# Attention scores of two heads issued as a pair: NSA and MoBA steps in a new order

## The chip, the cores and the metric

The kernel runs on one core of a Trainium2 chip. The metric is device time in microseconds (us). Three runs of the kernel before took 2022.54, 2023.51 and 2023.94 us, median 2023.51. The profiled execution took 2022.18 us; the span that the profile covers is 2020.5 us of it.

## The reference

The program computes two transformer blocks on 512 tokens of width 1024 in float32. Block one has a mixer of 8 NSA heads and 8 MoBA heads, then a mixture of 32 experts; block two has differential attention (DA) and retention. Cut to the branches that the change touches:

```python
# NSA, selected branch; with 8 selection blocks and a top of 16, every causal key is selected
s = einsum('bghcd,bgcmd->bghcm', qc, ksel) * scale
s = s - sl * dist
p = masked_softmax(s, dist >= 0)
o_sel = einsum('bghcm,bgcmd->bghcd', p, vsel)
# NSA, window branch: the same with kw, vw; the window of 512 covers all keys
return gc[..., 0:1] * o_cmp + gc[..., 1:2] * o_sel + gc[..., 2:3] * o_win
# MoBA, 8 heads, two key blocks of 256: causal attention over all keys
p = masked_softmax(concatenate([s_g, s_c]), concatenate([mask_g, mask_c]))
```

So in this kernel there are 16 causal attentions for NSA (8 heads, 2 branches) and 8 for MoBA, each with head width 64 and 512 queries.

## The kernel before, in words

A **step** is one block of 128 queries (row `i`, 0 to 3) of one head in one branch. It meets the first `i + 1` blocks of 128 keys. NSA has 64 steps and MoBA 32, numbered through (`st["at"]`). A step passes over three engines:

- TensorE (PE), `scores`: one matmul of 64 contracted partitions into one of three PSUM banks (`bank[n % 3]`), 128 to 512 columns wide. Queries and keys of a head lie in one half of the 128 partitions: `half` is 0 or 64. A float32 matmul shows as two records in the trace, so a step has two records of scores.
- VectorE (DVE), `dve_attend`: adds the bias and takes the row minimum in one pass (line 660), signal `s_bias`.
- ScalarE (ACT), `act_attend`: the exponential with its row sum (line 605), signal `s_exp`.
- PE, `turn`: transposes the probabilities, one block of 128 at a time (line 568), signal `t_done`. ACT copies them to SBUF (line 597), signal `t_ok`.
- PE, `values`: multiplies them with the values, one matmul a block (line 579), signal `o_done`.
- DVE, `accumulate`: reciprocal of the sum (line 641), in NSA times the gate (line 643), then the scaled addition into `omix` (line 648 in NSA, 651 in MoBA), signal `o_acc`.

Everything is written out by hand. `pe_attend` issues in its turn n: the scores of step n, the transposes of step n-2, the values of step n-3. `dve_attend` issues the bias of step m, then in NSA one piece of other work (`modulate_part`, line 629: an eighth of a chunk of the ada weights), then `accumulate` of step m-3. Both walk the lists `nsa_steps` and `moba_steps` in order. In the kernel before a head's four rows follow one another; heads of the two halves alternate head by head (0, 4, 1, 5, ... in NSA; even and odd in MoBA).

NSA steps are followed by the projections for MoBA (lines 395 and 403), then come the MoBA steps, the output projection (lines 789 and 798), the router, and the expert stage (lines 1426 and 1443), whose weights stream from HBM through a ring of 12 slots of 1 MB. In block two, `pe_da` issues the two score matmuls of a DA step (line 675), one in each half of the partitions, one directly behind the other.

Of the kernel before, what the change touches and what calls it, by code (L numbers as in the profile page):

```python
# [12 lines left out]
P = 128  # L13
S = 512
D = 1024
NT = S // P
# [3 lines left out]
HD = 64  # L20
HEADS = 8
# [52 lines left out]
def two_block_layer(nc, x, vec_rows_in, misc_in, ada_w, w_in, nsa_cmp_pos, nsa_cmp_w1, nsa_cmp_w2, w_out, router_w,  # L74
# [9 lines left out]
    with ExitStack() as ctx:  # L84
# [3 lines left out]
        def sem(name):  # L88
            return ctx.enter_context(nc.semaphore(name))

        bank = [ctx.enter_context(nc.psum_tensor(f"bank{i}", [P, 512], F32)) for i in range(8)]
# [17 lines left out]
        def room(at, shape, parts=P):  # L109
# [149 lines left out]
        s_done, s_bias, s_exp, t_done, t_ok, o_done, o_acc = (  # L259
            sem(n) for n in ("s_done", "s_bias", "s_exp", "t_done", "t_ok", "o_done", "o_acc"))  # L260
# [95 lines left out]
        at = norms = rs = 0  # L356
# [157 lines left out]
                    after[j["at"]]()  # L514


        nsa_steps, moba_steps, da_steps = [], [], []
        for br in range(2):
            for h in [0, 4, 1, 5, 2, 6, 3, 7]:
                half = HD * (h // 4)  # L520
                for i in range(NT):
                    nsa_steps.append(dict(
                        q=qkT[half:half + HD, h % 4, i * P:(i + 1) * P], k=qkT[half:half + HD, 4 + br, 0:P * (i + 1)],
                        v=lambda kt, br=br: vtok[:, kt, P * br:P * br + P], vw=HD, v0=half,
                        bias=bias8[:, h, S - P * (i + 1):S], blocks=i + 1,
                        over=nsa_gate[:, i, 3 * h + br + 1:3 * h + br + 2], dst=omix[:, i, HD * h:HD * h + HD], add=True))
        for h in range(HEADS):
            half = HD * (h % 2)
            for i in range(NT):
                moba_steps.append(dict(  # L530
                    q=qkT[half:half + HD, h // 2, i * P:(i + 1) * P], k=qkT[half:half + HD, 4 + h // 2, 0:P * (i + 1)],
                    v=lambda kt, h=h: vtok[:, kt, P * (h // 2):P * (h // 2) + P], vw=HD, v0=half,
                    bias=bias8[:, h, S - P * (i + 1):S], blocks=i + 1,
                    over=None, dst=omix[:, i, 512 + HD * h:512 + HD * h + HD], add=False))
        for h in range(4):
            for i in range(NT):
                da_steps.append(dict(
                    q=[qkT[HD * m:HD * m + HD, h, i * P:(i + 1) * P] for m in range(2)],
                    k=[qkT[HD * m:HD * m + HD, 4 + h, :] for m in range(2)],
                    v=lambda kt, h=h: vtok[:, kt, P * h:P * h + P],  # L540
                    bias=bias4[:, h, 384 - P * i:384 - P * i + S], dst=omix[:, i, P * h:P * h + P]))
        at = 0
# [7 lines left out]
        S_DA = O_MOBA + 2 * len(da_steps)  # L550

        def pe_attend(pe, steps, banks_free=None):
            def scores(st):
                n = st["at"]
                if n >= 3:
                    pe.wait_ge(s_bias, n - 2)
                pe.matmul(bank[n % 3][:, 0:P * st["blocks"]], st["q"], st["k"], start=True, stop=True)\  # L557
                  .then_inc(s_done, 1)

            def turn(st):  # L560
                n = st["at"]
                pe.wait_ge(s_exp, n + 1)
                if st is steps[0] and banks_free:
                    banks_free()
                if n >= 3:
                    pe.wait_ge(t_ok, n - 2)
                for b in range(st["blocks"]):
                    mm = pe.transpose(bank[3 + n % 3][:, b * P:(b + 1) * P], st["p"][:, b * P:(b + 1) * P],  # L568
                                      ident[:, :])
                mm.then_inc(t_done, 1)  # L570

            def values(st):
                n = st["at"]
                pe.wait_ge(t_ok, n + 1)
                if n >= 2:
                    pe.wait_ge(o_acc, n - 1)
                for b in range(st["blocks"]):

                    mm = pe.matmul(bank[6 + n % 2][:, 0:P], probT[n % 2][:, b * P:(b + 1) * P], st["v"](b),  # L579
                                   start=(b == 0), stop=(b == st["blocks"] - 1))  # L580
                mm.then_inc(o_done, 1)
            for n in range(len(steps) + 3):
                if n < len(steps):
                    scores(steps[n])
                if 2 <= n <= len(steps) + 1:
                    turn(steps[n - 2])
                if n >= 3:
                    values(steps[n - 3])
# [660 lines left out]
        def _(pe):  # L1249
# [86 lines left out]
            for g in range(2):  # L1336
                pe.wait_ge(c_ac, 5 + g)
                for i in range(NT):
                    mm = pe.matmul(bank[CMP_BANK[i]][:, SW * g:SW * g + SW], cmp_pT[:, g, P * i:P * i + P],
                                   vc_diag[:, g, :], start=True, stop=True)  # L1340
                    if g == 1:
                        mm.then_inc(c_pe, 1)

            pe_attend(pe, nsa_steps, lambda: pe.wait_ge(c_dv, C_O))
            pe.wait_ge(t_ok, O_NSA)
            pe.wait_ge(o_acc, O_NSA)
            pe_project(pe, moba_jobs,
                       after={moba_jobs[n]["at"]: lambda parts=parts: modulate(parts) for n, parts in MOD_AFTER.items()})
            pe.wait_ge(z_free, moba_jobs[-1]["at"] + 1)
            pe_attend(pe, moba_steps)  # L1350
            pe.wait_ge(o_acc, O_MOBA)
            pe_out(pe, 0, "w_out", 0)
# [736 lines left out]
```

## Time and profile before

| what | us |
|---|---|
| median of three runs | 2023.51 |
| profiled execution | 2022.18 |
| span in the profile | 2020.5 |
| NSA steps, from the first steady turn to the projections | 176.04 to 284.60 |
| MoBA steps | 389.13 to 442.50 |
| PE busy in the span | 1922.7 (95%) |
| DVE busy | 679.4 (34%) |
| ACT busy | 375.0 (19%) |

The PE row of the page is near 9 tenths nearly throughout. In a timeline row the second number is how long the group lasts by the profile, and the end of a matmul is modelled; the pace of an engine is read from one start to the next start. In the chain of waits a row's second number is the time that the row contributes to the chain, so these add up to elapsed time.

### The profile page before, as it was taken

To read this page: it belongs to the slowest core of one execution; us is meant where nothing else is said; L and a number is where in the kernel's file an instruction comes from. 1 tells how busy PE (TensorE), PEld (TensorE's weight loads), DVE (VectorE), ACT (ScalarE), POOL (GpSimd) and SP (SyncE) were. 2 spreads that over 40 slices of the span, in tenths; PEclk is the share of its full clock that TensorE was granted. 3 is DMA by queue.
4 is the path that set the end of the run, shared out by engine and by line. 5 is a ranking of instruction groups with operands and counts; after the bars stand their busy time and mean duration, and the time that the engine had idled before them with its cause. 6 is when DMAs were issued, how large, how long until landed. Compare 5 with 4: busy or idle time off the path is not lost.

```text
span 2020.5 us, 37108 instructions
## 1 busy us (share of the span) xinstructions
PE 1922.7 (95%) x15662; PEld 992.4 (49%) x15662; DVE 679.4 (34%) x1755; ACT 375.0 (19%) x821; POOL 192.3 (10%) x237
## 2 busy tenths in 40 slices
PE   5999999999799999999999998999999969989989
PEld 4486664764434434344434343434343434855854
DVE  6446767431412212121212121212121254176140
ACT  2214542250201101011101111111110112052010
POOL 1020000000002112012111111111111100000000
PEclk9979999999799999999999999999999989999999
DMA  9721223321289999999999999999999882100001
GB/s 303 219 80 54 73 78 110 132 93 63 75 317 382 393 397 400 397 396 391 398 398 393 399 395 397 402 387 369 391 395 401 339 267 90 63 1 1 1 0 42
DMA packets 144751, 498.97 MB, mean 247 GB/s; under 512 B 20787, under 2 KB 89513, under 8 KB 95433
## 3 DMA queue, kind: packets, MB, share of 16 engines
q1 hardware_dynamic: 122192, 464.81, 59.6%
q0 software_dynamic: 16448, 22.69, 5.3%
q10 hardware_dynamic: 5944, 9.09, 1.3%
q8 instruction: 125, 2.05, 0.4%
q14 instruction: 42, 0.34, 0.0%
HBM read 481.08 MB, written 17.96 MB: 247 GB/s over the span
## 4 chain that ended last, share of the span: by engine, by line
PE 83%; DMA 10%; DVE 4%; ACT 1%; issue 1%; SPq 1%; ACTq 0%; DVEq 0%
PE bank L1426 26%; PE bank L1443 12%; PE bank L395 10%; DMA ring<-in_exp_w_dram 9%; PE bank L403 8%; PE bank L798 6%; PE bank L557 3%; PE bank L579 3%; PE bank L568 2%; PE bank L1415 1%; PE bank L1407 1%; PE bank L769 1%; PE bank L379 1%; PE bank L1390 1%; DVE arena L745 1%; PE bank L1398 1%
## 5 line engine op out<-in xcount | busy, mean ns | idle before, releaser
L1426 PE MATMUL bank<-ring,arena 128*32 128x512 f32 x5568 | 646.6, 599 | 13.8 <-DMA ring<-in_exp_w_dram 11.7
L1426 PEld LDWEIGHTS bank<-ring,arena 128*32 128x32 f32 x5568 | 163.9, 110 | 327.4 <-issue 294.5
L1443 PE MATMUL bank<-ring,arena 128*32 128x256 f32 x5568 | 307.9, 379 | 7.7 <-DMA ring<-in_exp_w_dram 6.2
L1443 PEld LDWEIGHTS bank<-ring,arena 128*32 128x32 f32 x5568 | 181.8, 110 | 141.1 <-issue 22.0
L395 PE MATMUL bank<-hT,ring 128*128 128x512 f32 x448 | 210.3, 622 | 13.2 <-DVE hT L775 7.5
L1823 DVE COPY arena<-bank 128x12 f32<-128x12 f32 (+2 forms) x32 | 5.4, 170 | 558.8 <-PE bank L1390 545.0
L1037 POOL DMA_INDIRECT expert_sums<-arena,dst_r x85 | 131.7, 1549 | 403.9 <-ACT arena L1175 387.4
L403 PE MATMUL bank<-ring,hT 128*128 128x256 f32 (+1 forms) x768 | 156.4, 363 | 0.0
L395 PEld LDWEIGHTS bank<-hT,ring 128*128 128x128 f32 x448 | 87.7, 199 | 119.2 <-issue 115.9
L403 PEld LDWEIGHTS bank<-ring,hT 128*128 128x128 f32 x768 | 135.6, 190 | 18.4 <-issue 2.4
L1837 DVE TENSOR_TENSOR arena<-bank,arena 128x512 f32<-128x512 f32 x87 | 54.9, 684 | 190.8 <-PE bank L1426 190.8
L798 PE MATMUL bank<-hT,ring 128*128 128x512 f32 x256 | 113.0, 595 | 1.4 <-ACT hT L820 1.4
L1157 ACT ACTIVATE arena<-bank 128x384 f32<-128x384 f32 (+2 forms) x64 | 29.5, 462 | 363.3 <-PE bank L1407 363.1
L1028 POOL DMA_INDIRECT arena<-h_rows,src_i x32 | 32.8, 1026 | 592.8 <-PE bank L1407 422.0
L557 PE MATMUL bank<-arena 64*128 64x128 f32 (+1 forms) x192 | 76.1, 479 | 0.6 <-DVE arena L500 0.6
L798 PEld LDWEIGHTS bank<-hT,ring 128*128 128x128 f32 x256 | 47.7, 190 | 57.9 <-issue 56.0
L629 DVE SCALAR_TENSOR_TENSOR arena<-ring,vecs,arena 128x256 f32<-128x256 f32 x154 | 74.7, 485 | 3.5
L1175 ACT ACTIVATE arena<-bank,arena 128x256 f32<-128x256 f32 x85 | 34.5, 474 | 196.4 <-PE bank L1443 196.4
L1168 ACT ACTIVATE arena<-bank 128x384 f32<-128x384 f32 (+2 forms) x64 | 29.5, 462 | 220.5 <-PE bank L1415 196.0
L579 PE MATMUL bank<-arena 128*128 128x128 f32 x480 | 69.7, 276 | 0.0
L579 PEld LDWEIGHTS bank<-arena 128*128 128x128 f32 x480 | 62.4, 194 | 0.7 <-ACT arena L597 0.7
L605 ACT ACTIVATE arena<-arena,mn 128x128 f32<-128x128 f32 (+1 forms) x96 | 53.9, 562 | 33.6 <-DVE mn L660 31.9
(335 smaller groups left out, 1620.4 us busy)
## 6 DMA issues: line engine op xcount, KB each, us to landing
ring<-in_exp_w_dram SPq DMA_DIRECT2D x384, 1024.0 KB
ring<-in_ada_w_dram SPq DMA_DIRECT2D x24, 1024.0 KB
ring<-in_w_in_dram SPq DMA_DIRECT2D x23, 1024.0 KB
ring<-in_w_out_dram SPq DMA_DIRECT2D x8, 1024.0 KB
expert_sums<-arena POOLq DMA_DIRECT2D x5, 512.0 KB, 4.7
arena<-in_x_dram ACTq DMA_DIRECT2D x1, 2048.0 KB, 12.6
ring<-in_w_in_dram SPq DMA_DIRECT2D x8, 256.0 KB, 5.8
h_rows<-arena ACTq DMA_DIRECT2D x4, 512.0 KB, 3.3
```

Source lines behind the costliest of these rows:

```text
L395: mm = pe.matmul(z[:, :], w, hT[:, k, :], start=(k == 0), stop=(k == ND - 1))
L403: mm = pe.matmul(z[:, n * wd:(n + 1) * wd], hT[:, k, i * P:(i + 1) * P], chunk(j["name"], j["part"])[:, k, j["col"]:j["col"] + wd], start= ...
L557: pe.matmul(bank[n % 3][:, 0:P * st["blocks"]], st["q"], st["k"], start=True, stop=True)\
L568: mm = pe.transpose(bank[3 + n % 3][:, b * P:(b + 1) * P], st["p"][:, b * P:(b + 1) * P], ident[:, :])
L579: mm = pe.matmul(bank[6 + n % 2][:, 0:P], probT[n % 2][:, b * P:(b + 1) * P], st["v"](b), start=(b == 0), stop=(b == st["blocks"] - 1))
L605: act.activation(st["p"][:, 0:w], st["p"][:, 0:w], ACT.Exp, scale=-1.0, bias=mn[:, n % 4:n % 4 + 1], accum_out=ls[:, n % 4:n % 4 + 1]).the ...
L629: ins = dve.scalar_tensor_tensor(out=ada_sum[ch], in0=w, scalar=s, in1=ada_sum[ch], op0=ALU.mult, op1=ALU.add)
L798: mm = pe.matmul(bank[2 + n % 3][:, :], chunk(name, n // 2)[:, k, P * (n % 2):P * (n % 2) + P], hT[:, k, :], start=(k == 0), stop=(k == ND ...
L1037: pool.indirect_dma_start(y_quarters, bass.IndirectOffsetOnAxis(dst[:, g:g + 1], 0), ybuf[:, g, :], None, bounds_check=4 * (JUNK + CAP) - ...
L1426: mm = pe.matmul(bank[g][QUAD * c:QUAD * (c + 1), :].rearrange("p (h n) -> p h n", h=2), rowsT[:, k, QUAD * g:QUAD * (g + 1)], w[:, :, SW ...
L1443: mm = pe.matmul(bank[4 + g // 2][QUAD * c:QUAD * (c + 1), SW * (g % 2):SW * (g % 2 + 1)], actT[:, j, g, QUAD * q:QUAD * (q + 1)], w[:, c, :],
L1837: ins = dve.tensor_tensor(u_in[:, g, :], bank[g][:, :], b1_rows, ALU.add)
```

## The change

The lists of steps are made in another order: for a pair of heads, one in each half of the partitions, row 0 of both, then row 1 of both, and so on to row 3. Pairs are (t, t + 4) in NSA and (2t, 2t + 1) in MoBA. `pe_attend` issues the scores of steps n and n+1 together in even turns, behind one wait, and none in odd turns. The wait is the one that the second of them needs: its bank must have been read by the bias pass of step n-2. Transposes, values, and the programs of DVE and ACT keep their form; they follow the new order of the lists.

```diff
-            for h in [0, 4, 1, 5, 2, 6, 3, 7]:
-                half = HD * (h // 4)
-                for i in range(NT):
+            for i, h in [(i, h) for t in range(4) for i in range(NT) for h in (t, t + 4)]:
+                    half = HD * (h // 4)
...
-        for h in range(HEADS):
-            half = HD * (h % 2)
-            for i in range(NT):
+        for i, h in [(i, h) for t in range(4) for i in range(NT) for h in (2 * t, 2 * t + 1)]:
+                half = HD * (h % 2)
...
-            def scores(st):
-                n = st["at"]
+            def scores(a, b):
+
+                n = b["at"]
                 if n >= 3:
                     pe.wait_ge(s_bias, n - 2)
-                pe.matmul(bank[n % 3][:, 0:P * st["blocks"]], st["q"], st["k"], start=True, stop=True)\
-                  .then_inc(s_done, 1)
+                for st in (a, b):
+                    pe.matmul(bank[st["at"] % 3][:, 0:P * st["blocks"]], st["q"], st["k"], start=True, stop=True)\
+                      .then_inc(s_done, 1)
...
-                if n < len(steps):
-                    scores(steps[n])
+                if n < len(steps) and n % 2 == 0:
+                    scores(steps[n], steps[n + 1])
```

Below, PE's program early in NSA, before the change: the turns from the scores of 384 columns to the next ones of 128 (L557 scores, L568 transposes, L579 values; a row is a matmul, x3 three more alike).

```order
L557 MATMUL bank<-arena 128x384 [waits s_bias]
L568 MATMUL bank<-ident,arena 128x128 [waits t_ok,s_exp]
L579 MATMUL bank<-arena 128x128 [waits o_acc,t_ok]
L579 MATMUL bank<-arena 128x128 x3
L557 MATMUL bank<-arena 128x512 [waits s_bias]
L568 MATMUL bank<-ident,arena 128x128 [waits t_ok,s_exp]
L568 MATMUL bank<-ident,arena 128x128
L579 MATMUL bank<-arena 128x128 [waits o_acc,t_ok]
L557 MATMUL bank<-arena 128x128 [waits s_bias]
```

Between any two scores stand transposes and values, which use all 128 partitions, and each score has its wait for `s_bias`.

PE's program at the same place after the change, one pair of 512 columns up to the next pair of 128 (lines are one higher: L558 scores, L569 transposes, L580 values).

```order
L558 MATMUL bank<-arena 128x512 [waits s_bias]
L558 MATMUL bank<-arena 128x512
L569 MATMUL bank<-ident,arena 128x128 [waits t_ok,s_exp]
L569 MATMUL bank<-ident,arena 128x128 x2
L580 MATMUL bank<-arena 128x128 [waits o_acc,t_ok]
L580 MATMUL bank<-arena 128x128
L569 MATMUL bank<-ident,arena 128x128 [waits t_ok,s_exp]
L569 MATMUL bank<-ident,arena 128x128 x2
L580 MATMUL bank<-arena 128x128 [waits o_acc,t_ok]
L580 MATMUL bank<-arena 128x128 x2
L558 MATMUL bank<-arena 128x128 [waits s_bias]
L558 MATMUL bank<-arena 128x128
```

The second score of a pair stands directly behind the first and has no wait. Between two pairs stand the transposes of both steps of the pair before (here three blocks each), and the values of one step of the pair before that (two blocks) and one of the pair before (three blocks).

## Rows read from the trace of the kernel before

**Rows 1.** Page: busy time, and the chain that ended last, by engine.

```profile
PE 1922.7 (95%) x15662; PEld 992.4 (49%) x15662; DVE 679.4 (34%) x1755; ACT 375.0 (19%) x821; POOL 192.3 (10%) x237
...
PE 83%; DMA 10%; DVE 4%; ACT 1%; issue 1%; SPq 1%; ACTq 0%; DVEq 0%
```

**Rows 2.** Chain of waits, one head in NSA: start us, us, what.

```profile
230.91 1.05 PE bank L557 x2
231.97 0.37 PE bank L568 x2
232.33 0.22 PE bank L579 x2
232.56 0.42 PE bank L557 x2
232.97 0.48 PE bank L568 x3
233.45 0.45 PE bank L579 x4
233.90 0.63 PE bank L557 x2
234.53 0.59 PE bank L568 x4
235.11 0.67 PE bank L579 x6
235.78 0.84 PE bank L557 x2
236.62 0.26 PE bank L568
236.88 0.89 PE bank L579 x8
237.77 1.05 PE bank L557 x2
```

**Rows 3.** Chain of waits in MoBA, the same place in two heads.

```profile
402.85 1.05 PE bank L557 x2
...
409.71 1.05 PE bank L557 x2
```

**Rows 4.** Timeline of PE: one score of 512 columns in NSA, two in DA.

```profile
230.84 1.12 PE L557 MATMUL bank<-arena 64*128 64x512 f32 x2
...
1788.13 1.13 PE L675 MATMUL bank<-arena 64*128 64x512 f32 x4
```

**Rows 5.** Timeline in NSA, DVE: start us, us, engine, line, operation.

```profile
232.00 0.69 DVE L660 CUSTOM_DVE_ANT_0 arena<-bank,arena 128x512 f32<-128x512 f32 x1 [0.65 <-PE bank L557]
...
232.62 0.48 DVE L629 SCALAR_TENSOR_TENSOR arena<-ring,vecs,arena 128x256 f32<-128x256 f32 x1
...
233.02 0.16 DVE L641 RECIPROCAL cf<-ls 128x1 f32<-128x1 f32 x1
...
233.61 0.28 DVE L660 CUSTOM_DVE_ANT_0 arena<-bank,arena 128x128 f32<-128x128 f32 x1
...
233.81 0.48 DVE L629 SCALAR_TENSOR_TENSOR arena<-ring,vecs,arena 128x256 f32<-128x256 f32 x1
...
234.80 0.41 DVE L660 CUSTOM_DVE_ANT_0 arena<-bank,arena 128x256 f32<-128x256 f32 x1
...
235.13 0.48 DVE L629 SCALAR_TENSOR_TENSOR arena<-ring,vecs,arena 128x256 f32<-128x256 f32 x1
...
236.66 0.56 DVE L660 CUSTOM_DVE_ANT_0 arena<-bank,arena 128x384 f32<-128x384 f32 x1 [0.46 <-PE bank L557]
...
237.14 0.48 DVE L629 SCALAR_TENSOR_TENSOR arena<-ring,vecs,arena 128x256 f32<-128x256 f32 x1
```

**Rows 6.** Busy time by stretch: NSA, MoBA, router, DA.

```profile
core 0: us, PE busy (x) PEld busy (x) DVE busy (x) ACT busy (x) POOL busy (x), PEclk, DMA share, GB/s
176.04:284.60 108.56, 108.00 (x601) 72.99 (x602) 85.90 (x379) 65.70 (x190) 0.00 (x0) 1.00 0.24 75
389.13:442.50 53.37, 53.11 (x297) 35.96 (x297) 25.63 (x124) 31.70 (x94) 0.00 (x0) 1.00 0.37 153
520.00:550.00 30.00, 24.77 (x133) 16.67 (x132) 12.86 (x54) 9.02 (x19) 1.03 (x1) 0.73 0.21 81
1779.00:1822.00 43.00, 37.48 (x221) 22.75 (x220) 41.08 (x131) 29.56 (x75) 0.00 (x0) 1.00 0.00 1
```

## The prediction, made before the changed kernel had run

> **What bounds the kernel now.** I read the page first: PE is busy for 95% of the span and makes 83% of the chain that ended last [rows 1]. What PE is relieved of shortens the run if nothing else takes its place, so the question is what PE does in the stages that the change touches. The busy time by stretch answers it: PE is busy for 108.00 of 108.56 us in NSA and 53.11 of 53.37 us in MoBA, at a granted clock of 1.00, which is the 2.4 GHz level; DVE is busy for 85.90 and 25.63 us there, ACT for 65.70 and 31.70 us [rows 6]. The chain of waits, read in order of time, then shows that both stages are one repeated pattern. It stays on PE and takes 237.77 - 230.91 = 6.86 us for a head with four rows in NSA, and 409.71 - 402.85 = 6.86 us in MoBA [rows 2, 3]. That NSA, with a busier DVE, has the same period as MoBA says that DVE doesn't bind today.
>
> The four turns of such a period split into [rows 2]:
> - scores: 0.42, 0.63, 0.84, 1.05 us for 128 to 512 columns, 2.94 in all;
> - transposes: 0.26, 0.37, 0.48, 0.59 us for one to four blocks, 1.70 in all;
> - values: 0.22, 0.45, 0.67, 0.89 us, 2.23 in all.
>
> These add up to 6.87, the period within rounding.
>
> **What the change does to PE.** It leaves the number of matmuls as it is and places the scores of two heads, one in each half of the partitions, next to each other. This is worth something only if two such matmuls run at once. The trace has this case in another stage: in DA the two scores of a step, 512 columns each, one in each half, stand back to back. The timeline shows all four records within 1.13 us, where one lone score of 512 columns (two records) lasts 1.12 us [rows 4]. So the second matmul costs 0.01 us. DA has only this width; at 128 to 384 columns the bounds are nothing (both at once) and the full price of a second score, 0.42 to 0.84 us [rows 2]. I take 0.01 us at each width, since nothing in the pair depends on the width, and the row that shows a pair is nearest.
>
> The new unit of the pattern is eight steps: two heads, four rows. Before, it took 2 x 6.86 = 13.72 us. Now PE has scores 2.94 + 4 x 0.01 = 2.98, transposes 2 x 1.70 = 3.40, values 2 x 2.23 = 4.46: 10.84 us. Saved by PE: 2.88 us a unit. There are 8 units in NSA (16 heads and branches) and 4 in MoBA, so PE alone would allow 12 x 2.88 = 34.6 us.
>
> The Trainium skill has a less favourable figure. "TensorE: Matmul & The Clock Gate", section "Measured speedup vs the span model", gives 3.07 times the speed for four row tiles of 32, which is 77% of four. An estimate by that share would have a pair run 1.53 times as fast as two lone scores, so the unit's scores would take 2 x 2.94 / 1.53 = 3.84 us and some 0.9 us of each saving would be missing. The trace disagrees for two halves: 1.13 us for two against 1.12 for one is 1.98 times. I go by the trace.
>
> **MoBA.** Here DVE is busy for 25.63 of 53.37 us and ACT for 31.70 [rows 6]. Packed into 53.37 x 10.84 / 13.72 = 42.2 us they are at 61% and 75%, below PE. The saving is PE's, 4 x 2.88 = 11.5 us.
>
> **NSA.** Here the pace of DVE has to be set against PE's. From start to start [rows 5] the bias pass takes 232.62 - 232.00 = 0.62 us at 512 columns, 0.20 at 128, 0.33 at 256, 0.48 at 384. The piece of ada weights takes 233.02 - 232.62 = 0.40, and the three small operations of `accumulate` 233.61 - 233.02 = 0.59. A step is 0.99 us and its bias pass; eight steps are 8 x 0.99 + 2 x (0.20 + 0.33 + 0.48 + 0.62) = 11.18 us. That is above PE's 10.84. DVE becomes the bound in NSA, by a little, and the best unit is 11.18: a saving of 2.54, not 2.88.
>
> Whether 11.18 is reached depends on how evenly the two engines' work lies, because only three score banks stand between them. PE's work between the starts of two pairs is the pair's scores, the transposes of both steps of the pair before, and the values of one step of that pair and one of the pair before it (the listing of the change shows this). That is 0.43 + 1.18 + 0.67 + 0.89 = 3.17 us at 128 columns, 0.64 + 0.52 + 0.89 + 0.22 = 2.27 at 256, 0.85 + 0.74 + 0.22 + 0.45 = 2.26 at 384, and 1.06 + 0.96 + 0.45 + 0.67 = 3.14 at 512. DVE's work in the same four is 2.38, 2.64, 2.94 and 3.22 us. If no slack carried from one pair to the next the unit would be 3.17 + 2.64 + 2.94 + 3.22 = 11.97 us, a saving of 1.75. Nearly all of the gap is one place, the row of 128 columns, where PE has the heavy transposes of the row of 512 to finish. DVE comes into that place with a queue of its own, since it was behind in the three before, so most of the 0.79 us is absorbed. I take 11.3 us: 13.72 - 11.3 = 2.4 a unit, 8 x 2.4 = 19.3 us, with 14.0 and 20.3 us as the bounds.
>
> **The new wait.** A pair waits until the bias pass of step n-2 is done, where the first of its scores waited for step n-3. Queued behind it on PE are the transposes of step n-2, which need the exponential of that same step, later than its bias pass in any case. So the wait can hold up no transposes, only the pair. In the tightest place of the trace the bias pass at 512 columns started at 232.00 and lasts 0.69 us, so it is done at 232.69, and the scores two steps later began at 233.90 by the chain [rows 5, 2]: 1.2 us to spare. The saving of up to 1.05 us for a pair eats some of that, most in NSA where DVE is the later engine; this is the same coupling as above, priced there. ACT's and DVE's instructions are as many and as large as before.
>
> **Ends of the stages.** The first turns wait for the first bias pass and exponential as before, and the last steps drain one engine after the other. I take off 0.5 us for each stage, 1.0 in all (bounds 0 and 2).
>
> **What follows the stages** moves as a block. The expert stage could absorb time, since its weights stream. But just ahead of it, in the router, the DMA engines are at 0.21 and 81 GB/s [rows 6]: they wait for slots that PE frees, and these come as much earlier as the rest.
>
> Sum: 11.5 + 19.3 - 1.0 = 29.8 us. The profiled execution took 2022.2 us (span 2020.5 and 1.7 around it), which gives 1992.4. The median of the runs is 1.3 us higher: 2023.5 - 29.8 = 1993.7 us.
>
> **Rivals.**
>
> *DVE binds NSA harder.* The Trainium skill speaks for this in "TensorEngine Tiling (Array Packing)", section "PSUM Bottleneck": tiling speeds up TensorE and not the emptying of PSUM, which may become the limit. As a mechanism of this kernel: DVE, idle for 22.66 of 108.56 us [rows 6], loses this idle time, and any waits of its own that the pace from start to start hides cost the full time. With the unit at 11.97 us NSA saves 14.0, and the total is 11.5 + 14.0 - 1.0 = 24.5; with 0.1 us more for each of the 64 steps on top, 18.1. Time 1999 to 2005 us. For it: the two engines are within 4%. Against it: nothing in DVE's rows shows more than a short wait between dependent operations, and those are in the pace.
>
> *The pairs don't overlap here.* Then a pair costs two scores, PE's unit stays at 13.72 us, and the time is that of before, 2023 to 2025 us. For it: in NSA and MoBA the second score has no wait of its own, and the matmuls around are of all 128 partitions. Against it: in DA the neighbours are the same kind [rows 4], and a missing wait is no hindrance.
>
> *The expert stage takes the time back.* If the first experts' weights set its start and not the router, up to all 29.8 us would be lost: 1994 to 2023, with 2010 as the middle. Against it is the DMA share of 0.21 ahead of it [rows 6].
>
> *Slower: the clock of PE falls in NSA.* With DVE as the bound PE has gaps. In the router PE is busy for 24.77 of 30.00 us and the granted clock is 0.73 [rows 6], a mixture of the levels 2.4 and 1.2 GHz. If NSA ran at 1.2 GHz throughout, the unit would be 21.7 us, 8.0 more than before: 8 x 8.0 - 11.5 = 52 us slower, 2076 us. It decides once the clock share in NSA is below about 10.84 / (13.72 + 11.5 / 8) = 0.72. Against it: in DA PE is busy for only 37.48 of 43.00 us and the clock is 1.00 [rows 6]; in NSA I expect gaps of 3 to 4%.
>
> **Chances.** The forecast, a saving of 26 to 34 us: 0.68. DVE harder: 0.18. No overlap: 0.04. Taken back by the experts: 0.04. Clock: 0.03. The remaining 0.03 is a larger saving than PE's sum allows for the edges. A difference of 0.2%, 4 us, is about what a measurement can tell from none. Faster by more: 0.92; within it: 0.05; slower: 0.03. The range is 1988 to 2004 us: at the lower end PE's full 34.6 us, at the upper the harder DVE.
>
> **What would show it.** Right: the four records of a pair within 1.1 us at 512 columns and about 0.5 at 128; MoBA's unit near 10.8 us, all on PE; NSA's near 11.3 with DVE busy for nearly all of it, and the chain of waits there going over DVE (lines 661 and 630) for the first time; the clock at 1.00; the expert stage and all behind it as long as before and 30 us earlier. Wrong: the second score of a pair starting only when the first ends; PE waiting in every pair for the bias pass; a clock below 1.00 in NSA; a longer first expert.

## The result, and the profile after

The changed kernel takes 1988.87 us (median of four runs, 1988.11 to 1994.39) against 2023.72 for the kernel before: ratio 0.9835, 95% interval 0.982 to 0.985. When it was run once more beside other kernels, the medians were 1990.89 and 2023.80, ratio 0.9839 (0.9825 to 0.9852). The saving is 33 to 35 us. The forecast was a saving of 29.8 us, to 1993.7 us.

The page of the changed kernel, whose span is 1987.3 us: busy time and the chain by engine.

```profile
PE 1885.2 (95%) x15662; PEld 976.1 (49%) x15662; DVE 675.7 (34%) x1755; ACT 371.4 (19%) x821; POOL 192.3 (10%) x237
...
PE 78%; DMA 10%; DVE 8%; issue 2%; ACT 1%; SPq 1%; ACTq 0%; DVEq 0%
```

There are as many matmuls as before. PE has lost 37.5 us of busy time, and the chain has moved from PE (83% to 78%) to DVE (4% to 8%) [rows 1]. For where, the chain of waits in MoBA, one unit of eight steps of the changed kernel (L558 scores, L569 transposes, L580 values; x4 of L558 is a pair):

```profile
383.54 1.06 PE bank L558 x4
384.60 0.48 PE bank L569 x3
385.08 0.45 PE bank L580 x4
385.53 0.33 PE bank L569 x3
385.86 0.74 PE bank L580 x6
386.60 0.42 PE bank L558 x4
387.02 0.59 PE bank L569 x4
387.60 0.67 PE bank L580 x6
388.27 0.44 PE bank L569 x4
388.71 0.89 PE bank L580 x8
389.61 0.63 PE bank L558 x4
390.24 0.26 PE bank L569
390.50 0.89 PE bank L580 x8
391.39 0.11 PE bank L569
391.50 0.22 PE bank L580 x2
391.72 0.85 PE bank L558 x4
392.57 0.37 PE bank L569 x2
392.94 0.22 PE bank L580 x2
393.16 0.22 PE bank L569 x2
393.38 0.03 issue
393.41 0.71 PE bank L580 x4
394.12 1.06 PE bank L558 x4
```

Three things are to be seen beside [rows 2].
- A pair costs 1.06, 0.42, 0.63 and 0.85 us for its four records, at each width what a lone score cost (1.05, 0.42, 0.63, 0.84). The second score of a pair adds at most 0.01 us at any width.
- Transposes that follow scores cost 0.48, 0.59, 0.26 and 0.37 us, as before. Those that follow values cost 0.33, 0.44, 0.11 and 0.22: 0.15 us less each. In the kernel before all of them followed scores. Over the unit they are 2.80 us, not 3.40.
- The values are 4.79 us where 4.46 were expected: 0.74 instead of 0.67 in one place, and 0.71 instead of 0.45 in the last, behind 0.03 us of "issue" (time for which the profile shows no releaser). That PE waits there for the copy of the transposes is a reading, from the step's order; the chain does not name it.

The unit is 394.12 - 383.54 = 10.58 us against 13.72. In NSA the same view of the changed kernel shows another engine; here one step with a row of 384 columns, up to the bias pass of 512 columns.

```profile
236.43 0.55 DVE arena L661
...
236.99 0.40 DVE arena L630
237.39 0.09 DVE cf L642
...
237.49 0.17 DVE cf L644
...
237.72 0.17 issue
237.89 0.68 DVE arena L661
```

From one bias pass (L661) to the next, 237.89 - 236.43 = 1.46 us, the chain never leaves DVE. The 0.17 us of "issue" lies between the start of the scaled addition (L649) and that of the next bias pass. The timeline of PE gives the unit: pairs of 512 columns start at 213.52 and 224.74, 11.22 us apart.

```profile
213.52 1.13 PE L558 MATMUL bank<-arena 64*128 64x512 f32 x4
...
224.74 1.13 PE L558 MATMUL bank<-arena 64*128 64x512 f32 x4
```

Busy time by stretch of the changed kernel: NSA, MoBA, and the projections between them.

```profile
177.00:266.70 89.70, 86.51 (x600) 64.12 (x600) 83.00 (x378) 64.33 (x189) 0.00 (x0) 1.00 0.29 91
370.00:411.00 41.00, 40.80 (x294) 31.35 (x294) 24.68 (x121) 29.68 (x92) 0.00 (x0) 1.00 0.47 194
266.73:367.01 100.28, 100.28 (x348) 59.67 (x348) 57.35 (x107) 15.32 (x24) 0.00 (x0) 0.98 0.21 67
```

In NSA DVE is busy for 93% (79% before), PE for 96% and its clock stays at 1.00. To lay the whole difference out by stage, I take the starts of four groups in the chain of waits, first of the kernel before, then of the changed one: the pass ahead of NSA (L1728, L1729), the first projection (L395), the last one (L403), and the output projection (L798, L799).

```profile
172.30 1.74 DVE arena L1728 x3
...
284.61 8.82 PE bank L395 x20
...
372.58 13.94 PE bank L403 x64
...
448.65 14.00 PE bank L798 x32
```

```profile
173.24 1.73 DVE arena L1729 x3
...
266.73 8.82 PE bank L395 x20
...
353.07 13.94 PE bank L403 x64
...
417.44 14.00 PE bank L799 x32
```

| stretch | before | after | difference |
|---|---|---|---|
| ahead of NSA | 172.30 | 173.24 | +0.9 |
| NSA | 112.31 | 93.49 | -18.8 |
| projections | 87.97 | 86.34 | -1.6 |
| MoBA, with the last projection | 76.07 | 64.37 | -11.7 |
| from the output projection to the end | 1571.85 | 1569.86 | -2.0 |

The differences add up to 33.2 us, the difference of the two spans. 30.5 us of them lie in the two stages.

The first pair of 256 columns in NSA shows something that the kernel before does not have, a score that waits for a bias pass:

```profile
176.11 0.70 PE L558 MATMUL bank<-arena 64*128 64x256 f32 x4 [1.19 <-DVE mn L661]
```

In MoBA the same pair waits 0.49 us. It happens once at the start of each stage.

### The profile page after: what moved, and what is told of

The parts are those of the page before. It is cut to its first block, busy times and chain, and to the rows that moved or that the text cites. A ratio compares the mean times of both kernels' runs of the same rounds, so it can differ in the third digit from the quotient of the medians.

```text
span 1987.3 us, 37108 instructions
## 1 busy us (share of the span) xinstructions
PE 1885.2 (95%) x15662; PEld 976.1 (49%) x15662; DVE 675.7 (34%) x1755; ACT 371.4 (19%) x821; POOL 192.3 (10%) x237
## 4 chain that ended last, share of the span: by engine, by line
PE 78%; DMA 10%; DVE 8%; issue 2%; ACT 1%; SPq 1%; ACTq 0%; DVEq 0%
PE bank L1427 26%; PE bank L1444 12%; PE bank L395 10%; DMA ring<-in_exp_w_dram 9%; PE bank L403 8%; PE bank L799 6%; DVE arena L661 1%; PE bank L1416 1%; PE bank L1408 1%; PE bank L770 1%; PE bank L580 1%; DVE arena L630 1%; PE bank L379 1%; PE bank L1391 1%; DVE arena L746 1%
## 5 line engine op out<-in xcount | busy, mean ns | idle before, releaser
L395 PE MATMUL bank<-hT,ring 128*128 128x512 f32 x448 | 210.2, 621 | 13.2 <-DVE hT L776 7.5
L403 PE MATMUL bank<-ring,hT 128*128 128x256 f32 (+1 forms) x768 | 156.4, 363 | 0.0
L395 PEld LDWEIGHTS bank<-hT,ring 128*128 128x128 f32 x448 | 87.6, 199 | 119.1 <-issue 115.8
L403 PEld LDWEIGHTS bank<-ring,hT 128*128 128x128 f32 x768 | 135.6, 190 | 18.4 <-issue 2.4
L799 PE MATMUL bank<-hT,ring 128*128 128x512 f32 x256 | 113.0, 595 | 1.4 <-ACT hT L821 1.4
L799 PEld LDWEIGHTS bank<-hT,ring 128*128 128x128 f32 x256 | 47.7, 190 | 57.9 <-issue 56.0
L580 PE MATMUL bank<-arena 128*128 128x128 f32 x480 | 71.6, 282 | 0.5
L580 PEld LDWEIGHTS bank<-arena 128*128 128x128 f32 x480 | 61.4, 192 | 4.9 <-ACT arena L598 3.7
L606 ACT ACTIVATE arena<-arena,mn 128x128 f32<-128x128 f32 (+3 forms) x96 | 53.8, 560 | 49.7 <-DVE mn L661 47.7
L1164 ACT ACTIVATE arena<-arena 128x768 f32<-128x768 f32 (+2 forms) x32 | 25.1, 786 | 167.1 <-DVE arena L1841 167.1
```

Of the source, the lines that this page charges most:

```text
L395: mm = pe.matmul(z[:, :], w, hT[:, k, :], start=(k == 0), stop=(k == ND - 1))
L403: mm = pe.matmul(z[:, n * wd:(n + 1) * wd], hT[:, k, i * P:(i + 1) * P], chunk(j["name"], j["part"])[:, k, j["col"]:j["col"] + wd], start= ...
L606: act.activation(st["p"][:, 0:w], st["p"][:, 0:w], ACT.Exp, scale=-1.0, bias=mn[:, n % 4:n % 4 + 1], accum_out=ls[:, n % 4:n % 4 + 1]).the ...
L799: mm = pe.matmul(bank[2 + n % 3][:, :], chunk(name, n // 2)[:, k, P * (n % 2):P * (n % 2) + P], hT[:, k, :], start=(k == 0), stop=(k == ND ...
```

## Experiments

**Pairs in the same half.** Does the gain come from the two halves, or from issuing two scores together? This kernel pairs heads of one half.

```diff
-            for i, h in [(i, h) for t in range(4) for i in range(NT) for h in (t, t + 4)]:
+            for i, h in [(i, h) for t in (0, 2, 4, 6) for i in range(NT) for h in (t, t + 1)]:
...
-        for i, h in [(i, h) for t in range(4) for i in range(NT) for h in (2 * t, 2 * t + 1)]:
+        for i, h in [(i, h) for t in (0, 1, 4, 5) for i in range(NT) for h in (t, t + 2)]:
```

> Pairs are issued back to back as in the changed kernel, but both heads of a pair lie in the same half of the partitions: (0,1), (2,3), (4,5), (6,7) in NSA and (0,2), (1,3), (4,6), (5,7) in MoBA. Theory A (the two scores run at once in the two halves, and besides PE saves about 0.15 us wherever transposes follow values instead of scores): the scores of a unit go back up from 2.96 us by 2.1 to 2.9 us, so MoBA's unit of eight steps is 12.7 to 13.5 us, and the time 2009 to 2020 us. Rival B (what helps is the bundling and the single wait, not the halves): as the changed kernel, MoBA's unit 10.6 us, 1989 us.

Measured: 2015.04 us, ratio to the kernel before 0.9958 (0.9941 to 0.9974). The timeline of PE in this kernel, two pairs of 512 columns a unit apart:

```profile
404.50 1.98 PE L558 MATMUL bank<-arena 64*128 64x512 f32 x4
...
417.21 1.98 PE L558 MATMUL bank<-arena 64*128 64x512 f32 x4
```

The pair takes 1.98 us instead of 1.13, and the unit 12.71 us. Theory A holds, and rival B falls as the account of the whole gain; a smaller part of it stays, as the next lines show. The chain of waits of this kernel gives the four pairs:

```profile
417.29 1.91 PE bank L558 x4
...
421.19 0.64 PE bank L558 x4
...
424.41 1.06 PE bank L558 x4
...
426.95 1.48 PE bank L558 x4
```

They are 5.09 us against 2.96 for pairs over two halves: 2.13 us is what the overlap of the halves is worth in a unit, and 12.71 - 10.58 = 2.13 is the difference of the units. The other 1.01 us of the gain (13.72 to 12.71) comes with pairing as such: the second score in the same half costs 2.15 us over the four widths where a lone one costs 2.94, a saving of 0.79; the transposes behind values save 0.60; the longer values and the issue seen above give back 0.36. These are sums of rows in the chain; no kernel tries one of the three alone.

Twelve units of 1.01 would be 12.1 us; the ratio allows 5 to 12, and the medians differ by 8.1. By stage, in the profiled execution, NSA is 7.4 us shorter than in the kernel before (104.92 against 112.31 us). MoBA is 1.1 us longer (77.18 against 76.07), since a stretch at the lower clock fell into its first unit, which takes 15.76 us from pair to pair (388.74 to 404.50) instead of 12.71. The granted clock from 380 to 404 us is 0.79:

```profile
380.00:404.00 24.00, 22.81 (x103) 15.46 (x102) 10.11 (x50) 10.80 (x36) 0.00 (x0) 0.79 0.86 351
```

This is not the clock rival of the prediction, which needs PE to be short of work because of DVE: PE is busy for 22.81 of the 24.00 us, and DVE for 10.11. The other kernels start MoBA behind a similar gap (in the changed one PE is busy for 8.87 of the 10 us from 360) and stay at 1.00 there. What set the clock down is open.

**The new order without pairs.** The lists as in the changed kernel, the scores as in the kernel before.

```diff
-                if n < len(steps) and n % 2 == 0:
-                    scores(steps[n], steps[n + 1])
+                if n < len(steps):
+                    single(steps[n])
```

> The new order of the steps (the two heads of a pair in turn, row by row), but each score issued in its own turn with its own wait as before. Theory A: nothing overlaps, PE's unit is 13.72 us as before, the time 2022 to 2025 us. Rival B' (the order alone evens out the engines' work or changes other waits): a part of the gain, 2000 to 2018 us.

Measured: 2021.23 us over ten runs (2018.48 to 2031.56), ratio 0.9997 (0.9982 to 1.0013). Two first scores of 512 columns a unit apart, from its chain of waits:

```profile
394.04 1.05 PE bank L565 x2
...
407.75 1.05 PE bank L565 x2
```

13.71 us against 13.72: the order by itself does nothing for the unit. In time, the interval allows 4 us less to 3 us more than before, so the median, 0.8 us under the expected 2022 to 2025, says no more. Theory A holds.

**NSA alone, and MoBA alone.** Each keeps the other stage as it was (`nsa_steps` in pairs and `moba_steps` single, and the reverse).

```diff
-                if n < len(steps) and n % 2 == 0:
-                    scores(steps[n], steps[n + 1])
+                if steps is nsa_steps:
+                    if n < len(steps) and n % 2 == 0:
+                        scores(steps[n], steps[n + 1])
+                elif n < len(steps):
+                    single(steps[n])
```

> Only the NSA steps in pairs; MoBA's order and scores as before. Theory A, by the stage of the two traces: 18.8 us less than before, 2005 us (2003 to 2007, since stretches at the lower clock around the stage can move). If the stages depended on each other the sum of this and of the MoBA-only kernel would differ from the whole gain of 34.9 us by more than 4.

> Only the MoBA steps in pairs; NSA's order and scores as before. Theory A: 11.7 us less than before, 2012 us (2010 to 2014). With the NSA-only kernel this shows whether the 4 us that the two stages don't account for belong to one of them or to the shift of what lies behind.

Measured: NSA alone 2001.15 us, ratio 0.9893 (0.9877 to 0.991), MoBA alone 2013.19 us, ratio 0.9944 (0.9928 to 0.9961). That is 21.6 us (18 to 25) and 11.3 us (8 to 15), together 33 us, the whole gain within the scatter, so nothing speaks for a dependence of the stages on each other beyond some 4 us. The NSA-only kernel came out 1.9 us under the 2003 to 2007 us that I had expected. 1.6 us of its gain lie in the projections behind NSA (86.34 us against 87.97), as in the changed kernel; the MoBA-only kernel does not have them (87.99) and came out where expected, between 2010 and 2014 us. In the timelines the units are those of the changed kernel: in the first one NSA's pairs of 512 columns start at 201.15 and 212.38 (11.23 us); in the second one MoBA's are 10.58 us apart:

```profile
404.04 1.13 PE L558 MATMUL bank<-arena 64*128 64x512 f32 x4
...
414.62 1.13 PE L558 MATMUL bank<-arena 64*128 64x512 f32 x4
```

**Less work for DVE in NSA.** Is NSA's 11.22 us DVE's? The ada piece beside each step covers 16 columns of 256 (but for the first of a chunk), so most of these sums are left out and the output is another. Only the call is shown; `modulate_part` takes the width as an argument.

```diff
-                modulate_part(dve, EARLY_DVE * ND + m)
+                modulate_part(dve, EARLY_DVE * ND + m, 16)
```

> The changed kernel, but the piece of ada weights that DVE works on beside each NSA step covers 16 of 256 columns (but for the first piece of a chunk), so that part of the adaLN sums is left out and the output differs. DVE's step loses some 0.2 us or more. Theory A (DVE binds NSA now, 11.21 us a unit, and PE's own work there is MoBA's 10.58): NSA's unit falls to 10.6 us, 5 us less for the stage, 1984 us. Rival C (11.21 us is PE's or a latency of the three-engine chain, DVE's load doesn't matter): the unit stays at 11.2, 1989 us.

Measured: 1987.09 us (1984.27 to 1989.28), ratio 0.9817 (0.9802 to 0.9832). Its timeline in NSA:

```profile
200.95 1.13 PE L558 MATMUL bank<-arena 64*128 64x512 f32 x4
...
211.53 1.13 PE L558 MATMUL bank<-arena 64*128 64x512 f32 x4
```

The unit is 10.58 us, to the hundredth MoBA's. DVE was the bound. In time the kernel is 1.8 us ahead of the first median of the changed one and 3.8 ahead of the one taken beside it, where 5 were expected; the runs scatter by 5 us, so the unit is the sharper evidence. By stage, NSA is 5.4 us shorter than in the changed kernel taken beside it (88.19 against 93.59 us), and the projections behind it are 1.7 us longer (87.99 against 86.34).

**One reciprocal and one gate product for a pair.** The same relief for DVE with nothing left out: on even steps both columns are done in one instruction, on odd steps neither.

```diff
-                dve.wait_ge(s_exp, n + 1)
-                link(dve.reciprocal(c, ls[:, n % 4:n % 4 + 1]))
-                if st["over"] is not None:
-                    link(dve.tensor_tensor(c, st["over"], c, ALU.mult))
+                if n % 2 == 0:
+                    c2 = cf[:, n % 4:n % 4 + 2]
+                    dve.wait_ge(s_exp, n + 2)
+                    link(dve.reciprocal(c2, ls[:, n % 4:n % 4 + 2]))
+                    if st["over"] is not None:
+                        link(dve.tensor_tensor(c2, st["over2"], c2, ALU.mult))
```

Here `over2` holds the gates of heads h and h + 4, which lie 12 columns apart.

> The changed kernel, with DVE's reciprocal and gate product done once for both steps of a pair (two columns in one instruction) instead of for each: two small operations, about 0.39 us by their starts, less for each pair, 1.56 us a unit in NSA. Theory A: DVE's unit in NSA is 9.6 us, below PE's, so the unit becomes PE's 10.6 us; 8 x 0.6 = 5 us less than the changed kernel, 1984 us. Rival C: unit stays at 11.2 us, 1989 us. Against both: the first accumulate of a pair now waits for the second step's exponential too; if that is late, DVE waits and the unit rises, up to 11.5 us, 1991 us.

Measured over five runs: 1985.48 us (1984.55 to 1986.76), ratio 0.9811 (0.9798 to 0.9825). This is the fastest kernel of the study. Its timeline in NSA, and its busy time there:

```profile
202.06 1.13 PE L559 MATMUL bank<-arena 64*128 64x512 f32 x4
...
212.64 1.13 PE L559 MATMUL bank<-arena 64*128 64x512 f32 x4
```

```profile
176.00:262.00 86.00, 84.71 (x604) 64.15 (x604) 76.10 (x321) 65.82 (x192) 0.00 (x0) 1.00 0.30 94
```

The unit is 10.58 us again, and both stages now have PE's. The feared wait for the second exponential does not show in the unit.

**The changed kernel once more**, beside the two last.

> The changed kernel once more, beside the others on the same chip, since single runs scatter by some 3 us. By all theories 1988 to 1990 us, NSA's unit 11.21 us and MoBA's 10.58.

Measured over five runs: 1990.89 us (1990.59 to 1993.38), 0.9 us above the expected 1988 to 1990, and 5.4 us above the batched kernel on the same chip, where 8 x (11.22 - 10.58) = 5.1 was to be expected. The runs of the two don't meet. In the profiled executions NSA accounts for 5.3 us of it (93.59 against 88.27), and the projections run 1.7 us the other way (86.34 against 88.01). Its profiled execution spanned 1991.7 us against 1987.3 of the first one, by the same program.

## Why the prediction was right, step by step

- *What bounds it.* PE bound both stages, and what PE saved came out of the span, in NSA up to the point where DVE became the bound. Shown.
- *Two halves run at once, 0.01 us for the second score.* Right at all four widths: the unit's scores are 2.96 us, 2.98 forecast. But the prediction's premise, that the new places are worth something only if two such matmuls run at once, was wrong. In one half, without overlap, the unit still fell from 13.72 to 12.71 us and the time by 8 us, because the second of two adjacent scores costs 0.79 us less over the four widths than a lone one, and transposes behind values cost less. The overlap itself is worth 2.13 of the 3.14 us saved in a unit, not the 2.88 that the prediction put down to it, and the rival without overlap, 2023 to 2025 us, was priced too high. The estimate by the Trainium skill's figure for four row tiles ("TensorE: Matmul & The Clock Gate", "Measured speedup vs the span model"), 3.84 us, does not hold for two halves; the row of DA was the better source.
- *PE's unit.* This is the term that was mis-sized: 10.84 us forecast, 10.58 measured, 11.7 us of stage time in MoBA where 11.0 were forecast. I had carried over the transposes at 3.40 us. Half of them now follow values and cost 0.15 us less each, 2.80 in all; the longer values and the 0.03 us of issue took back 0.36. The 0.15 us was not visible before, since every group of transposes there followed scores. What matches it is the change from matmuls of 64 contracted partitions to those of 128. The Trainium skill ("TensorEngine Tiling (Array Packing)", "Key Properties") says that changing the tiling mode drains TensorE, and gives no price; the trace is in keeping with it, at 0.15 us. That the drain is the cause, and not some other cost of following scores, no run here isolates.
- *NSA's unit.* 11.3 us forecast, 11.22 measured, a stage saving of 18.8 us as forecast. DVE's sum of 11.18 from the starts of its instructions was nearly exact, and the unevenness cost 0.04 us, not the 0.8 of the upper bound. The two kernels with a lighter DVE show that it is the bound. The Trainium skill ("TensorEngine Tiling (Array Packing)", "PSUM Bottleneck") warns that the emptying of PSUM may become the limit once TensorE is faster; the trace agrees in that the engine that reads the scores out of PSUM became the bound, though what was taken off it in the two kernels was other work. The rival that drew on this, DVE binding harder by the unevenness and by hidden waits, did not occur.
- *The new wait.* Right for the steady steps, wrong at the start of each stage. The prediction gave a spare 1.2 us, read from a steady place, and let the first turns go "as before". At the start the second pair waits 1.19 us in NSA and 0.49 us in MoBA for the bias pass of the step before it, where no score in the kernel before waits for one.
- *Ends of the stages.* Sized too low: in NSA 8 x (13.72 - 11.22) = 20.0 less the measured 18.8 leaves 1.2, in MoBA 4 x 3.14 = 12.6 less 11.7 leaves 0.9. That is 2.1 us where 1.0 was forecast, just outside the stated bounds of 0 and 2. The new wait at the start of each stage is the part of it that the trace names. That NSA's 18.8 us came out exactly is luck in this sense: the unit was 0.08 us shorter than forecast, eight times, and the ends took it back.
- *What follows moves as a block.* Right, and a little more: 2.7 us beyond the two stages (3.6 behind them, less 0.9 ahead of NSA). 1.6 are in the projections, which hold one stretch at a lower granted clock: 0.83 in the 10 us from 280 in the changed kernel, 0.66 in the 10 us from 300 in the kernel before. From one kernel to the next this goes with NSA. In the three profiles in which DVE bounds NSA (changed, the same once more, NSA-only) the projections up to L403 take 86.34 us each; in the six in which PE does, they take 87.97 to 88.01, also in the batched kernel and the one with less ada work, where NSA ends earliest. So it seems to be an after-effect of PE's gaps in NSA, and the batched kernel gives it back; no run isolates that. The other parts scatter without a pattern, though their code is the same: from the output projection to the end 1569.86 to 1573.57 us over the nine profiles (1571.85 in the kernel before), and 172.07 to 173.89 ahead of NSA. The expert stage absorbed nothing beyond that scatter.
- *Rivals.* No overlap: refuted by the pairs' four records and by the kernel with pairs in one half. Slower clock in NSA: 1.00 in every NSA stage seen, though one kernel met a low stretch in MoBA.

The measured time is 4.8 us under the forecast, and at the second measurement 2.8. The first lies within the stated range by 0.9 us only, and its saving of 34.9 us is above the 26 to 34 us to which the prediction gave its main chance, and above PE's full 34.6; the second, 32.9 us, is inside. In the profiled execution the saving was 33.2 us, 3.4 more than forecast: 0.7 from the two stages, where the smaller unit outweighed the larger ends, and 2.7 from outside them. Of these the 1.6 of the projections came back each time that DVE bound NSA, and the other 1.1 are within the scatter of parts that did not change. So the lower median owes something to luck: one program showed 4.4 us between two profiles.

## What to carry to other kernels

Attention heads of width 64 that lie in the two halves of the partitions should have their score matmuls issued directly one behind the other: here the second was free, and grouping alone, without the halves, was worth a third of the gain in a unit (1.01 of 3.14 us). Before counting on it, add up the other engines' unit by the starts of their instructions, since a faster PE can hand the bound to the next, and look at the first turns of a stage apart from the steady ones. When VectorE becomes the bound, the same pairing that helped PE lets small per-row operations of VectorE be done two at a time.

## What the runs showed of the hardware

- Two score matmuls in different halves take 1.13 us at 512 columns (changed kernel), in the same half 1.98 (pairs in the same half), alone 1.12 (kernel before).
- Even in the same half the second of two is cheaper than the first: 1.91 - 1.05 = 0.86 us at 512 columns and 0.64 - 0.42 = 0.22 at 128.
- A group of transposes costs 0.15 us more behind 64-partition scores than behind 128-partition values, whatever its size from one block to four (changed kernel, chain of waits).
- On VectorE a reciprocal or a product of two columns takes 0.16 us (batched kernel), and of one column 0.16 us as well (changed kernel).
